# Two fused transformer blocks, the last residual: the input of the last addition is stored ahead and accumulating transfers add the rest

## The reference

```python
h2 = modulate(rmsnorm(x, g_pre2[l]), sh2, sc2)
x = x + gt2 * rmsnorm(conv_ffn(h2, w_up[l], conv_w[l], conv_b[l], w_down[l]), g_post2[l])
```

## Time and profile before

| | |
|---|---|
| median of 3 runs | 1379.78 us (1378.79 to 1381.59) |
| the profiled execution's own time | 1379.42 us |
| its span, first to last instruction | 1377.6 us |
| what lies around the span | 1.8 us |
| PE busy in the span | 1352.9 us (98%) |
| DVE, ACT, POOL busy | 842.9, 634.5, 27.0 us |
| granted clock of PE, mean | 0.999 |
| last matmul of w_down ends | 1365.39 us |
| last ACT copy to X ends | 1374.44 us |

### The profile page before, as it was taken

One profiled execution on the slowest core, in us unless ns is written; L12 is line 12 of the kernel. 1 busy time (PEld: TensorE's weight loads), 2 busy tenths in 40 slices (PEclk: granted clock), 3 DMA queues, 4 the chain that ended last, 5 costly groups with the idle time before them and its releaser, 6 DMA issues.

```text
span 1377.6 us, 17051 instructions
## 1 busy us (share of the span) xinstructions
PE 1352.9 (98%) x6768; PEld 1099.3 (80%) x6768; DVE 842.9 (61%) x1286; ACT 634.5 (46%) x1034; POOL 27.0 (2%) x28
## 2 busy tenths in 40 slices
PE   9999998999999999999999999999999999999998
PEld 6777665788888888888986777887898888888888
DVE  7577897487866767755886544357765344344334
ACT  7435667554455444333645444444544333333334
POOL 3000000000003000000000000000000000000000
PEclk9999999999999999999999999999999999999999
DMA  7524221323222223664031111134313223223221
GB/s 252 192 92 138 77 77 32 123 108 122 94 91 100 98 92 116 235 208 160 32 131 61 56 53 61 62 123 138 138 62 106 93 92 105 95 92 106 94 92 62
DMA packets 46202, 146.62 MB, mean 106 GB/s; under 512 B 4875, under 2 KB 11915, under 8 KB 45740
## 3 DMA queue, kind: packets, MB, share of 16 engines
q1 hardware_dynamic: 45836, 145.02, 31.0%
q10 hardware_dynamic: 288, 0.52, 0.1%
HBM read 142.12 MB, written 3.41 MB: 106 GB/s over the span
## 4 chain that ended last, share of the span: by engine, by line
PE 87%; DVE 7%; ACT 3%; issue 1%; DMA 1%; SPq 0%; DVEq 0%; ACTq 0%
PE PS L352 26%; PE PS L353 25%; PE PS L354 25%; PE PS L1054 1%; PE PS L1045 1%; PE PS L1020 1%; DVE wlo L318 1%; DVE X L1718 1%; DVE Hlo L1718 1%; PE PS L567 1%; PE PS L919 1%; PE PS L719 1%; PE PS L656 1%; ACT whi L302 1%; DVE macc L1718 1%
## 5 line engine op out<-in xcount | busy, mean ns | idle before, releaser
L318 DVE TENSOR_TENSOR wlo<-raw,whi 128x1024 fp32r<-128x1024 f32 x202 | 248.3, 1233 | 334.7 <-ACT whi L302 334.0
L352 PE MATMUL PS<-Hhi,whi 128*128 128x512 f32 (+1 forms) x1136 | 430.8, 379 | 7.6 <-DVE Hlo L1718 4.3
L354 PE MATMUL PS<-Hhi,wlo 128*128 128x512 f32 (+1 forms) x1136 | 422.3, 372 | 0.0
L353 PE MATMUL PS<-Hlo,whi 128*128 128x512 f32 (+1 forms) x1136 | 422.2, 372 | 0.0
L302 ACT ACTIVATE whi<-raw 128x1024 fp32r<-128x1024 f32 x202 | 212.0, 1054 | 241.7 <-DMA raw<-in_w_down 116.5
L352 PEld LDWEIGHTS PS<-Hhi,whi 128*128 128x128 f32 x1136 | 214.0, 188 | 56.8 <-issue 10.7
L354 PEld LDWEIGHTS PS<-Hhi,wlo 128*128 128x128 f32 x1136 | 214.0, 188 | 37.8
L353 PEld LDWEIGHTS PS<-Hlo,whi 128*128 128x128 f32 x1136 | 214.1, 188 | 35.1 <-issue 0.2
L352 PE MATMUL PS<-Dhi,whi 128*128 128x512 f32 (+1 forms) x384 | 142.9, 372 | 0.0
L353 PE MATMUL PS<-Dlo,whi 128*128 128x512 f32 (+1 forms) x384 | 142.6, 371 | 0.0
L354 PE MATMUL PS<-Dhi,wlo 128*128 128x512 f32 (+1 forms) x384 | 142.6, 371 | 0.0
(11 more groups left out here) (409 smaller groups left out, 1811.4 us busy)
## 6 DMA issues: line engine op xcount, KB each, us to landing
raw<-in_w_up SPq DMA_DIRECT2D x88, 512.0 KB, 3.5
wm<-in_w_mod SPq DMA_DIRECT2D x48, 512.0 KB, 4.1
raw<-in_w_down SPq DMA_DIRECT2D x44, 512.0 KB, 3.5
raw<-in_w_g SPq DMA_DIRECT2D x16, 512.0 KB, 3.4
raw<-in_w_out SPq DMA_DIRECT2D x8, 512.0 KB, 3.6
raw<-in_w_o SPq DMA_DIRECT2D x8, 384.0 KB, 3.4
raw<-in_w_sv SPq DMA_DIRECT2D x4, 512.0 KB, 4.2
raw<-in_w_dv SPq DMA_DIRECT2D x4, 512.0 KB, 4.8
```

Source lines behind the costliest of these rows:

```text
L318: e.tensor_tensor(wlo[i % NS], raw[i % NS], whi[i % NS].bitcast(f32), ALU.subtract).then_inc(q["w_lo"], 1)
L352: e.matmul(o, lhs[0], rhs[0], start=first, stop=False, skip_group_check=own)
L353: e.matmul(o, lhs[0], rhs[1], start=False, stop=False, skip_group_check=own)
L354: return e.matmul(o, lhs[1], rhs[0], start=False, stop=last, skip_group_check=own)
```

## The change

- SP: after the load of the second block's w_up chunk 16 (counted from 0) it stores the whole of `X` (2 MB) to the output, once the addition that makes it is done (`x_new`, reached long before). At the end it only waits. The eight stores of the result are gone.
- DVE: `residual` is replaced by `update`, one operation in place: Y_A = Y_A * P2 * G_r, for all 16 half blocks. DVE also adds the first six squares of half b into G_s (`down_sums_b`, five additions), between the updates of half a. The order of updates is a0 to a5, then b0 to b5, a6, a7, b6, b7.
- PE: three matmuls with ones for half b where there were eight; the twelve with the identity are gone.
- ACT: the six copies from PSUM to X are gone.
- POOL: nine transfers from its queue, with addition to what the output holds, each waiting for the updates of its blocks: a0-1, a2-3, a4-5, b0-1, b2-3, b4-5, a6-7 of 256 KB, then b6 and b7 of 128 KB.

```diff
@@ sync_program
+        load_to(e, ld, CH["w_up2"] + 12 + NS)
+        e.wait_ge(q["x_new"], XN[3])
+        e.dma_start(out, X).then_inc(q["l_res"], 16)
         load_to(e, ld, NCHUNK)
-        for c in range(0, 8, 2):
-            e.wait_ge(q["x_new"], XN[3] + c + 2)
-            e.dma_start(out[:, c:c + 2, HALF["a"]], X[:, c:c + 2, HALF["a"]]).then_inc(q["l_out"], 16)
-        for c in (0, 2, 6, 4):
...
-            e.dma_start(out[:, c:c + 2, HALF["b"]], X[:, c:c + 2, HALF["b"]]).then_inc(q["l_out"], 16)
-        e.wait_ge(q["l_out"], 128)
+        e.wait_ge(q["l_res"], 16)
+        e.wait_ge(q["l_out"], 144)
@@ tensor_program
-        for i in range(8):
+        e.wait_ge(q["p_acc"], PA[3] + 7 + 5)
+        e.matmul(PS[:, 6, HALF["b"]], ones, G_s[:, HALF["b"]], start=True, stop=False)
+        for i in (6, 7):
             e.wait_ge(q["p_sq"], SQ[3] + 8 + i + 1)
-            last = e.matmul(PS[:, 6, HALF["b"]], ones, sq_p[i][:, HALF["b"]], start=i == 0, stop=i == 7)
+            last = e.matmul(PS[:, 6, HALF["b"]], ones, sq_p[i][:, HALF["b"]], start=False, stop=i == 7)
         last.then_inc(q["stat"], 1)
-
-        e.wait_ge(q["x_new"], XN[3])
-        e.wait_ge(q["p_y"], PY[3] + 15)
-        for c in range(N_PE):
-            e.matmul(PS[:, c, HALF["b"]], ident, X[:, c, HALF["b"]], start=True, stop=False)
-        for c in range(N_PE):
-            e.wait_ge(q["p_w"], c + 1)
-            e.matmul(PS[:, c, HALF["b"]], ident, v_pe[c], start=False, stop=True).then_inc(q["x_pe"], 1)
@@ scalar_program
-        for c in range(N_PE):
-            e.wait_ge(q["x_pe"], c + 1)
-            act(X[:, c, HALF["b"]], PS[:, c, HALF["b"]], ACT.Copy, "x_out")
@@ vector_program
-        for c in range(8):
-            residual(3, "a", c, P2)
+        def update(h, c):
+            y = Y_A[:, c, HALF[h]]
+            stt(y, y, P2[:, c:c + 1], G_r[:, HALF[h]], ALU.mult, ALU.mult, "p_w")
+
+        e.wait_ge(q["r"], RS["p3a"])
+        update("a", 0)
+        for c in range(1, 3):
+            down_sums_b(1, c, c + 1)
+            update("a", c)
+        down_sums_b(1, 3, 6)
+        for c in range(3, 6):
+            update("a", c)
         e.wait_ge(q["r"], RS["p3b"])
-        for c in range(N_PE):
-            stt(v_pe[c], Y_A[:, c, HALF["b"]], P2[:, c:c + 1], G_r[:, HALF["b"]], ALU.mult, ALU.mult, "p_w")
-        for c in range(N_PE, 8):
-            residual(3, "b", c, P2, XN[3] + 8 + c - N_PE)
+        for c in range(6):
+            update("b", c)
+        for h in "ab":
+            for c in (6, 7):
+                update(h, c)
@@ gpsimd_program
+        e.wait_ge(q["l_res"], 16)
+        for h, c, n, count in (("a", 0, 2, 2), ("a", 2, 2, 4), ("a", 4, 2, 6), ("b", 0, 2, 8), ("b", 2, 2, 10),
+                               ("b", 4, 2, 12), ("a", 6, 2, 14), ("b", 6, 1, 15), ("b", 7, 1, 16)):
+            e.wait_ge(q["p_w"], count)
+            e.dma_start(out[:, c:c + n, HALF[h]], Y_A[:, c:c + n, HALF[h]], accum_op=ALU.add).then_inc(q["l_out"], 16)
```

More of the change, by code:

```diff
@@ L166, in build @@
     n_v = [[G_a, G_b, sq_m[3]], [G_a, G_b, sq_m[14]]]
-    N_PE = 6
-    v_pe = [sq_m[8 + c][:, 0:256] for c in range(N_PE)]
     sq_p = [G_s, G_b, G_a, G_c, G_d, sq_m[0], sq_m[1], sq_m[2]]
```

## The result

The changed kernel takes **1383.07 us** (median of 12, 1381.19 to 1386.27) against 1379.53 for the kernel before, timed beside it: a ratio of **1.0031** (95% interval 1.0021 to 1.0040), 3.5 us at the medians (some 4.3 by the ratio) slower. The forecast was 1380.2, in a range of 1377.3 to 1385.3: no change as the likeliest case, slower at 0.33.

The account below looks back on a forecast made before the run. PE bounds the kernel until w_down's last matmul; 12.2 us of computing and draining follow. Computing -2.56 us, drain from 3.2 to 6.1, net +0.4 on the 1379.78 median: 1380.2 us, range 1377.3 to 1385.3.

Parts of the forecast that it names:

- r of half a: Near the end, ACT's Exp for half a, ended at 1362.04; its result releases DVE for half a's updates at 1362.14.
- The store ahead: SP's 2 MB store of X among the w_up loads, where PE is full: at most 8 us delay, cost 0.
- The computing part: After w_down's last matmul, 9.05 us before the change; predicted to end 2.56 us earlier, at 1371.88 instead of 1374.44.
- the drain: From end of computing to end of span, while output transfers finish: predicted to grow from 3.2 to 6.1 us.
- the rival of a long issue on POOL: At the end, POOL's one-by-one issuing sets the bound: +2.76 us at 1.6 us per issue, +5.5 at 2; chance 0.23.
- The start of b0-1: Half b's first adding transfer: ready at 1368.72, data moving at 1370.2 after 1.1 us issue and 0.35 us.
- G: POOL's time to issue one transfer at the end: taken as 1.1 us, between bounds 0.50 and 1.69.
- The rate: Adding transfers at the end: 185 GB/s, from a 400 GB/s load and a 345 GB/s store in sequence.
- The ending: After the last byte moves at 1377.3: landing 0.4 us later, span end 0.3 us after that, at 1378.0.
- DVE holding POOL up: POOL makes no transfers during half b's updates, starting on them at 1371.88: +2.6 us or more, about 1383; chance 0.07.
- Cheap all round: At the end, issues under 0.72 us and 300 GB/s or more: faster, down to 1376.0 us; chance 0.10.
- below 138 GB/s: Rival at the end: accumulation slower than this rate makes the kernel slower; chance 0.04 together with weights held up.

Follow-up runs that it names:

- the mixtures: Kernel before with five sums moved to DVE and 6, 4 or 0 half-a blocks added by POOL's transfers: 1377.06, 1378.12, 1379.62 us; kernel before beside them 1377.71.

## Why the prediction was right or wrong

Counted from r of half a, the prediction's steps against the profile after:

| step | predicted | measured |
|---|---|---|
| last matmul with ones ends | 4.81 | 5.14 |
| DVE starts half b | 5.80 | 6.11 |
| last update ends | 9.84 | 10.16 |
| POOL takes up b0-1 | 6.68 | 7.30 |
| b0-1 begins to move | 8.16 | 9.55 |
| full rate ends | 15.26 | 17.35 |
| span ends | 15.96 | 19.15 |

*Right.* The store ahead costs nothing that can be told (alone: 1.0007, interval around 1, and no pause of PE). The computing part gains: predicted 2.56 us, measured 2.24 in the profile, the whole tail being 2.9 shorter with plain stores from SP. Of the 0.3 us in the first rows, 0.1 is the sums, which take 0.53 each where one needs the one before, instead of 0.47; the rest is the six matmuls with ones, 1.55 us instead of 1.30, since the first two, with no other one before them, take 0.67. The transfers, not POOL, set the end, and the changed kernel pays at the drain more than it gains in computing.

*Partly luck.* The time lies in the range, but above the forecast's own, 1377.3 to 1382.5, and slower by more than the 0.2% that I called no change and gave 0.57. The part of the range that holds it, up to 1385.3, was there for the rival of a long issue on POOL, and that is not what made the kernel slow.

*Where it failed: the size of the drain*, 6.1 us predicted, 9.0 measured. Three terms make up the 3.2 us of the whole:
- The start of b0-1, 1.4 us late. I gave POOL no time to take up a semaphore; it takes 0.3 (update ends 1371.54, issue 1371.85). From the start of an issue to its first data I took 1.45, G and the stores' 0.35; from POOL the first data of all move some 1.9 us after the issue starts. DVE's 0.3 is in it too, and some 0.35 for the rest of a4-5: half a's transfers were through 9.5 us after r of half a, where I had 7.5.
- The rate, 0.7 us. 168 GB/s against the 185 that I worked out from a load and a store one behind the other. The rule that I set beside it, half the rate of a copy (the Trainium skill, Collectives: The Full Stack, section "The bandwidth ceiling: the fold count and why AG ≠ RS ≠ AR"), gives 345/2 = 172, and the steady part agrees at 168. With pieces of 8 KB it was 209, above what the rule gives, so the agreement does not show that the rule is the reason.
- The ending, 1.1 us. From the end of the full rate to the end of the span I took 0.7, as for the stores; it took 1.8: stragglers until about 1382.6 in the profile's clock, SP's wait until 1383.1, and POOL's own drain until 1383.45 before the engines part.

*The rivals.* POOL's issuing as the bound is refuted: the transfers had no gaps, and 0.71 MB moved after 1378, when POOL had only its last 0.13 MB to make. My sum has a slip there: at G = 1.6 the end is +2.5 us, not yet the 2.76 of the 0.2%, which takes 1.65. G was 1.11 in the mean of the six and up to 1.35, near the 1.1 that I took as the middle of two far bounds: a lucky pick. DVE holding POOL up does not show: POOL takes up b0-1 0.31 after its semaphore and makes it in 1.19, with DVE in its row of ten updates until 1374.71. "Cheap all round" is refuted: plain stores from POOL met its conditions (an issue of 0.70, over 300 GB/s) and still gained only 1.5 us (0.9989) of the 2.8 that it asks for, and adding ones met neither. Adding stayed below 138 GB/s only in the ramp and the dips; from 1368 to 1374, with both in it, the mean is 129.

## What to carry to other kernels

Price the stretch after the last computation as a pipeline of its own: pick-up, first data, bytes over rate, landing, the queue's own drain. An adding transfer there ran here at half a store's rate (168 against 345 GB/s), and cost about a microsecond more at its start and at its end; the same transfer beside computing freed DVE for 1.8 us of tail (16.4 to 14.6), more than it cost. So give the early blocks to it and leave the last ones to a plain store, and check that the two do not meet. And look at the granted clock before you believe a difference of a microsecond.

## What the runs showed of the hardware that was not expected

- Adding to HBM from SBUF in rows of 1 KB ran at 168 GB/s in its steady part, stores of the same rows at about 345; pieces of 8 KB added at 209.
- A plain transfer of this shape takes POOL 0.73 to 0.88 us to issue, in packets of 4 KB, and an adding one 1.19 to 1.35 with nothing before it in the row, in packets of 1 KB (SP: 0.4 to 0.5 a store, in packets of 1 KB).
- The first adding transfers of a run ramp up slowly: 41 to 137 GB/s in the first microsecond, and a dip to 34 to 90 before the second.
- The time of one kernel goes with its mean granted clock, with nothing else changed: beside the mixtures the kernel before takes 1377.0 to 1377.7 us at 1.000 and 1381.4 to 1382.7 at 0.996. In the two profiles that I compared 2.5 us of this kind were there in the first 250 us, so the tails had to be compared from a common event.
